# Row stores by block, an earlier load of the first token group, and a new place for row sums in a one-layer streaming encoder

## What is computed

```python
h = _rmsnorm(y, norm1_g)
fq, fk, fv, logf, gq, gk, gv, glog, gr = _project(h, w_in, ...)   # one combined projection
fox_o = _fox_prompt(fq, fk, fv, logf)        # forgetting attention, 8 heads
gla_o, S = _gla_prompt(gq, gk, gv, glog)     # gated linear attention, 4 heads
y = y + _merge(fox_o, gla_o, gr, gla_norm_g, w_out)
y = y + (silu(n @ w_gate) * (n @ w_up)) @ w_down      # n = _rmsnorm(y, norm2_g), D_FF = 2816
```

## Time and profile before

| | us |
|---|---|
| median of 3 runs | 3261.18 (3258.51 to 3264.07) |
| profiled execution, own time | 3258.25 |
| its span | 3256.5 |
| PE busy in the span | 2992.0 (92%) |
| DVE / ACT / POOL busy | 2127.7 / 1476.5 / 1332.9 |
| mean granted TensorE clock | 0.958 |

### The profile page before, as it was taken

How to read it: one execution, slowest core, us unless ns; L and a number is a source line. 1 busy time by engine, 2 the same in 40 slices (tenths; PEclk the granted TensorE clock), 3 DMA queues, 4 the chain that set the end, 5 groups by cost and what they waited for, 6 DMA issues and landing times. The chain is left out here.

```text
span 3256.5 us, 56218 instructions
## 1 busy us (share of the span) xinstructions
PE 2992.0 (92%) x21017; PEld 2761.5 (85%) x21017; DVE 2127.7 (65%) x3916; ACT 1476.5 (45%) x2998; POOL 1332.9 (41%) x1115
## 2 busy tenths in 40 slices
PE   7999998969999968599996999999999999999997
PEld 5899998957778746377775999999999999999997
DVE  6142333428999954577773777787778867787766
ACT  6253111117888842254453444444444544454443
POOL 1010033400000000322213777777778677777773
PEclk9999999989999989699997999999999999999999
DMA  5234577753332234333334655556555575556552
GB/s 127 72 126 175 192 236 247 217 123 73 75 78 59 57 88 186 108 120 120 126 111 133 186 154 148 146 150 199 146 149 150 146 209 149 146 150 183 164 148 72
DMA packets 526644, 459.52 MB, mean 141 GB/s; under 512 B 42969, under 2 KB 462102, under 8 KB 517312
## 3 DMA queue, kind: packets, MB, share of 16 engines
q1 hardware_dynamic: 510680, 402.53, 43.1%
q0 software_dynamic: 14352, 49.03, 4.6%
q10 hardware_dynamic: 1344, 4.36, 0.6%
HBM read 353.36 MB, written 102.47 MB: 140 GB/s over the span
## 5 line engine op out<-in xcount | busy, mean ns | idle before, releaser
L2605 PE MATMUL ps_ffn<-hop,wop 128*128 128x260 f32 x7392 | 985.9, 285 | 20.9 <-POOL hop L2263 17.0
L2605 PEld LDWEIGHTS ps_ffn<-hop,wop 128*128 128x128 f32 x7392 | 934.1, 191 | 22.5 <-issue 22.5
L2617 PE MATMUL ps_ffn<-aT,dsp 128*128 128x260 f32 x4224 | 599.9, 285 | 30.0 <-DVE yacc L2449 22.1
L702 PE MATMUL ps_project<-hT,wsp 128*128 128x416 f32 (+1 forms) x3000 | 603.7, 357 | 0.0
L2617 PEld LDWEIGHTS ps_ffn<-aT,dsp 128*128 128x128 f32 x4224 | 546.7, 190 | 36.8 <-issue 27.2
L702 PEld LDWEIGHTS ps_project<-hT,wsp 128*128 128x128 f32 (+1 forms) x3000 | 549.0, 186 | 24.1 <-issue 8.7
L2255 POOL TENSOR_TENSOR wop<-wsum_n,wop 128x512 fp32r<-128x512 f32 x352 | 483.0, 1372 | 134.4 <-ACT wop L2289 132.8
L2255 POOL TENSOR_TENSOR wop<-wraw_n,wop 128x512 fp32r<-128x512 f32 x264 | 362.0, 1371 | 231.3 <-ACT wop L2289 231.2
L2449 DVE TENSOR_TENSOR yacc<-ps_ffn,yacc 128x260 f32<-128x260 f32 x640 | 267.1, 422 | 142.5 <-PE ps_ffn L2617 142.0
L2289 ACT ACTIVATE wop<-wsum_n 128x512 fp32r<-128x512 f32 x352 | 222.0, 631 | 245.3 <-PE ps_ffn L2605 244.6
L2289 ACT ACTIVATE wop<-wraw_n 128x512 fp32r<-128x512 f32 x264 | 166.0, 629 | 175.5 <-PE ps_ffn L2605 165.9
(11 more groups left out here) (278 smaller groups left out, 4248.5 us busy)
## 6 DMA issues: line engine op xcount, KB each, us to landing
wsum_n<-wsum SPq DMA_DIRECT2D x352, 256.0 KB, 5.0
draw<-in_w_down_dram SPq DMA_DIRECT2D x88, 512.0 KB, 3.5
wraw_n<-in_w_gate_dram SPq DMA_DIRECT2D x132, 256.0 KB, 3.6
wraw_n<-in_w_up_dram SPq DMA_DIRECT2D x132, 256.0 KB, 3.6
zT<-zs SPq DMA_DIRECT2D x12, 1040.0 KB, 4.0
wraw<-in_w_in_dram SPq DMA_DIRECT2D x24, 512.0 KB, 5.8
hraw<-h2T SPq DMA_DIRECT2D x16, 520.0 KB, 9.0
qk_hi<-work SPq DMA_DIRECT2D x8, 1024.0 KB, 4.4
```

Source lines behind the costliest of these rows:

```text
L702: last = pe.matmul(ps[0:w, p % NB, 0:BLK], wsp[:, b, s, k, 0:w], hT[:, g * TPB:(g + 1) * TPB, v, k, :], start=k == 0 and m == 0, stop=k == ...
L2605: last = pe.matmul(product_bank(c, i), wop[:, i, w, k, :], hop[:, i, v, k, :], start=k == 0 and m == 0, stop=k == KH - 1 and m == 2)
L2617: last = pe.matmul(ps[:, 6 + n % 2, 0:FH], dsp[:, h, w, f, c * P:(c + 1) * P], aT[:, u % 2, x, f, t * FH:(t + 1) * FH], start=f == 0 and m ...
```

## The change

Three parts.

1. project: store_rows stores a tile block by block. It waits for the copy of one block, stores this block's four token tiles (three in the last block), and goes on to the next; the two tails of 72 and 32 rows follow the last block. There are five semaphores in place of one, and out_rows(n, g) waits for the store of the same block g of the tile before.
2. gla_merge and ffn: the four loads of the first group's normed rows are issued in gla_merge's loop at t = 9, behind store_h(7), and no longer at the head of ffn's queue. hraw and its semaphores live in a scope around both stages, which clears them at its end; the buffer wst shares x2's place.
3. ffn: in every up cell (s = 1) silu of J12 stands behind item 2 and not ahead of C11, and make_a of J22 behind item 4. At the three turns, sum_h of T2 stands behind item 2, low_h of T2 ahead of low_a of J11, and sum_h of T4 behind make_a of J21.

```diff
-        r_stored = sem("r_stored")
+        r_stored = [sem(f"r_stored{g}") for g in range(NB)]
...
             def store_rows(n, prompt, sample, c):
-                sp.wait_ge(rows_out, NB * (n - N_ROWS + 1))
-                full = (NT - 1) * TT
-                sp.dma_start(prompt[0:full, c:c + P].rearrange("(t p) c -> p t c", p=TT),
-                             zr[:, 0:NT - 1, :]).then_inc(r_stored, 16)
-                sp.dma_start(prompt[full:SEQ, c:c + P], zr[0:LAST_PROMPT, NT - 1, :]).then_inc(r_stored, 16)
-                sp.dma_start(sample[:, c:c + P], zr[LAST_PROMPT:TT, NT - 1, :]).then_inc(r_stored, 16)
+                for g in range(NB):
+                    sp.wait_ge(rows_out, rows_index(n, g) + 1)
+                    t0, t1 = g * TPB, min((g + 1) * TPB, NT - 1)
+                    sp.dma_start(prompt[t0 * TT:t1 * TT, c:c + P].rearrange("(t p) c -> p t c", p=TT), zr[:, t0:t1, :]).then_inc(r_stored[g], 16)
+                sp.dma_start(prompt[(NT - 1) * TT:SEQ, c:c + P], zr[0:LAST_PROMPT, NT - 1, :]).then_inc(r_stored[NB - 1], 16)
+                sp.dma_start(sample[:, c:c + P], zr[LAST_PROMPT:TT, NT - 1, :]).then_inc(r_stored[NB - 1], 16)
...
             def out_rows(n, g):
                 r = rows_index(n, g)
-                if g == 0:
-                    if n > N_ROWS:
-                        dve.wait_ge(r_stored, 48 * (n - N_ROWS))
-                    else:
-                        dve.wait_ge(p_n_stored, 48)
+                if n > N_ROWS:
+                    dve.wait_ge(r_stored[g], (48 if g == NB - 1 else 16) * (n - N_ROWS))
+                elif g == 0:
+                    dve.wait_ge(p_n_stored, 48)
...
                 if t >= 2:
                     store_h(t - 2)
+                if t == 9:
+                    sp.wait_ge(h_stored, 16 * (-(-FT // CH) + 1))
+                    for b in range(4):
+                        load_group(sp, d, 0, b)
                 if 1 <= t <= NCH:
                     store_x(t - 1)
...
             load_w(0, P1)
-            load_h(0, 0)
             load_w(0, P5)
-            load_h(0, 1)
             load_w(0, P6)
-            load_h(0, 3)
             load_w(0, P2)
-            load_h(0, 2)
...
                     if turn:
                         low_h(q, O_T1)
-                        sum_h(q, O_T2)
                     combine(c, U2)
                     combine(c, V2)
-                    silu(u, J12)
                     combine(c, C11)
                     item(c, 2)
+                    if turn:
+                        sum_h(q, O_T2)
+                    silu(u, J12)
                     item(c, 3)
                     make_a(u, J11)
                     combine(c, U3)
                     combine(c, C22)
+                    item(c, 4)
                     make_a(u, J22)
-                    item(c, 4)
-                    low_a(u, J11)
                     if turn:
                         low_h(q, O_T2)
-                        sum_h(q, O_T4)
+                    low_a(u, J11)
                     item(c, 5)
                     combine(c, C21)
                     make_a(u, J21)
+                    if turn:
+                        sum_h(q, O_T4)
                     low_a(u, J22)
```

More of the change, by code:

```diff
@@ L297, in _ @@
             sp.wait_ge(t_stored[1], 16 * 6)
-            sp.wait_ge(r_stored, 48 * NTR)
+            for g in range(NB):
+                sp.wait_ge(r_stored[g], (48 if g == NB - 1 else 16) * NTR)
             sp.wait_ge(halves_stored, 32 * 8)
@@ L1406, in gla_merge @@
         grow = sb("grow_m", [P, D])
-        wst = sb("wst", [P, 2, D])
         wsp = sb("wsp_m", [P, 2, KD, D], F32R)
@@ L1411, in gla_merge @@
         x2 = sb("x2s", [P, 2, D])
+        wst = x2
         xn = sb("xn_m", [P, D])
@@ L2063, in late_row, with load_group @@
     return items_before(NCELL) + 2 * ITEMS + (r if r >= 4 else 3 * r + 2 - ITEMS)
+def load_group(sp, d, q, b):
+    k, t = divmod(b, 2)
+    tok = q * FT + t * FH
+    sp.dma_start(d["hraw"][:, KH * k:KH * (k + 1), FH * t:FH * (t + 1)], d["h2T"][:, KH * k:KH * (k + 1), tok:tok + FH])\
+        .then_inc(d["h_come"][b], 16)
 def ffn(nc, d):
@@ L2071, in ffn @@
         grow = sb("grow_n", [TT, D])
-        hraw = sb("hraw", [P, KD, FT])
+        hraw = d["hraw"]
         hop = sb("hop", [P, NPROD, 2, KH, FH], F32R)
@@ L2094, in ffn @@
         filled, g_in = sem("filled_n"), sem("g_in_n")
-        h_come = [sem(f"h_come{b}") for b in range(4)]
+        h_come = d["h_come"]
         h_hi, h_low_v, h_low_p, h_sum = sem("h_hi_n"), sem("h_low_v"), sem("h_low_p"), sem("h_sum")
@@ L2171, in load_h @@
             def load_h(q, b):
-                k, t = divmod(b, 2)
-                if q and b == 0:
+                if b == 0:
                     sp.wait_ge(h_low_v, 3 * q)
@@ L2178, in load_h @@
                         sp.wait_ge(y_stored[r], 16 * (q - 1))
-                tok = q * FT + t * FH
-                sp.dma_start(hraw[:, KH * k:KH * (k + 1), FH * t:FH * (t + 1)], d["h2T"][:, KH * k:KH * (k + 1), tok:tok + FH])\
-                    .then_inc(h_come[b], 16)
+                load_group(sp, d, q, b)
             def load_x(q, t):
@@ L2687, in stream_step @@
     fox_sample(nc, d)
-    gla_merge(nc, d)
-    ffn(nc, d)
+    with ExitStack() as ctx:
+        sb, sem, _ = scope(nc, ctx)
+        d["hraw"] = sb("hraw", [P, KD, FT])
+        d["h_come"] = [sem(f"h_come{b}") for b in range(4)]
+        gla_merge(nc, d)
+        ffn(nc, d)
 _INS = ['x_prompt', 'x_sample', 'cache_fox_k', 'cache_fox_v', 'cache_fox_logf', 'state_gla', 'norm1_g', 'w_in', 'w_gate2',
```

## The result

The changed kernel takes 3230.23 us (median of 5 runs, 3227.11 to 3231.28) against 3261.64 us beside it: a ratio of 0.9903, 95% interval 0.9888 to 0.9917, 31.4 us less. Forecast were 3238 us, 23 less, and a range of 3225 to 3252. The sign, the range and the larger half of the working were right; the sum is short by 8 us, and one term of it was wrong in kind.

The account below looks back on a forecast made before the run. PE, busy in 92% of the span, was taken as the bound, so gains come from its idle or slow-clock time. Terms -16 - 3.5 + 0 - 4.5 + 0 + 0.7 = -23.3 us gave 3238 us at the median, range 3225 to 3252.

Parts of the forecast that it names:

- The row stores: In project, block stores remove PE's waits for row copies, then the weight-sum chain is next: -16 us (-20 to -6).
- the 20 us at stake: In project, PE's waits for row copies plus slow matmuls behind them, without the last wait at the end: 20 us.
- The lower price that the text set for the chain, 2.3 us: In project, the weight-sum chain at 10.1 us a step takes back 2.3 us; at 10.9, all 20.
- The end of project: After the last copy only the last block and tails remain to store, so the next stage starts sooner: -3.5 us.
- The head of ffn: Group 0 loaded early lets DVE's sums stand ready and shrinks POOL's 4.08 us pause: -4.5 us (-2 to -7).
- The regular cells: In ffn's regular up cells PE has no waits, DVE's work is unchanged and no add comes later: 0.
- The turns: At ffn's three turns waits move on one item; DVE's tail limits PE's win to 1.5 us each: 0 (-4.5 to +4.5).
- The added scope: Around gla_merge and ffn, clearing semaphores and meeting once more at the end costs +0.7 us (0 to 1.5).
- The sums bind: Rival, project: weight-sum step falls only from 11.2 to 10.9 us, project wins 7 us; 3247 us, chance 0.18.
- The turns pay: Rival, ffn's turns: DVE and POOL alternate better, DVE's tail shrinks, 10.5 us gained over three turns; 3227 us, chance 0.09.
- The early load does nothing: Rival, head of ffn: the weights' landing alone holds POOL and ACT, start moves by 0.5 us; 3242 us, chance 0.05.
- Slower by small pieces: Rival, project: store pieces beside every weight-sum step slow it to a mean of 12.2 us, +23 us; 3277 us, chance 0.06.

Follow-up runs that it names:

- part 1 alone: Kernel before with only the block-by-block row stores of project (all of the diff to do with r_stored): 3239.03 us, ratio 0.9915.
- part 3 alone: Kernel before with only DVE's new order in ffn, in up cells and at the three turns: 3262.44 us, ratio 0.9986.
- part 2 alone: Kernel before with only the early load of group 0's rows in gla_merge, with its scope: 3263.26 us, ratio 0.9986.
- the run with one line moved: Kernel before with only item 4's add put ahead of make_a of J22 in the up cells: 3256.80 us, ratio 0.9964.
- 52 KB: Changed kernel with each row store split into pieces of one token tile, 22 transfers per tile in place of 7: 3229.39 us, ratio 0.9883.

## Why the prediction was right, and where it was not

**The row stores.** Right in mechanism: the stalls went, the chain of weight sums was next, at the step that was forecast (10.2 us, forecast 10.1). The term was mis-sized: of the 20 us at stake 4 were given to the chain, and it took none here (project -21.7 at PE's last transpose) and 2.8 us in the execution of part 1 alone. DVE's lateness of 9 us that PE bears without a wait was in the working, but not trusted. The lower price that the text set for the chain, 2.3 us, was nearer. The stake was too small as well: it was read from one trace. In the five kept traces with one store per tile PE waits 18.4 to 22.0 us, and its last transpose in project ends at 696.95 to 702.70; the trace of before is the lowest in both. The longest waits are those of the run with part 3 alone:

```profile
PE ps_project L714 <- DVE zr L528: 22.0, 9, 7.3
```

In the nine with stores by block it ends at 674.44 to 678.09. The means are 23.5 us apart. Together with the next term that is 29 us, and part 1 alone gave 28, where 19.5 were forecast: this is more than all of the 8 us that the sum was short by.

**The end of project.** Also mis-sized, 3.5 where 5.2 were measured. By the formula of the Trainium skill ("DMA: Bandwidth & Descriptors", Anatomy of one DMA — SWDGE (gpsimd) path) the estimate was 5.7, nearer than mine; the page gives it for transfers that GpSimd issues, and these are SP's. Part of the gain, nearly 2 us, has a cause that was not in the working: the store itself became faster in pieces.

**The head of ffn.** 4.5 forecast, 3.3 in the trace of after, 4.6 (by its ratio) for part 2 alone. The bound named, POOL's pause of 4.08 us, is the place where it went.

**The regular cells.** The step that failed reads: "In regular up cells PE has no waits; DVE's work is the same, and no add comes later. 0." It asked only whether an add comes later, and not whether one comes sooner where PE waits for it. PE started item 6 late by 0.16 us and P3 by 0.07 more, in half or all of the up cells, below what the list of waits shows. In the run with one line moved make_a of J22 still takes 1.29 to 1.31 us in most regular cells, beside a POOL step that began 0.28 us earlier, and all of these cells have the short pitch: it is the add's place that counts, not make_a's length. The line gives 12 us by the ratio (7.5 to 15.7 by its interval), 4 to 8.5 by the traces; that the runs of before mostly waited in all up cells would fit both, but no trace of them is kept. In the pair of traces above the regular cells give 2.9 of the 28.5 us.

**The turns.** 0 was forecast, with the two waits moved by an item, and a tail that lets PE win at most 1.5 us. The moved wait came as forecast (3.15 us at item 5), and the tail too: DVE's adds of items 0 and 1 came no sooner. But the first turn's cost in after is the same as before to 0.4 us, and the third's 1.7 us more: +1.6 in all, within the bounds. A third wait, for low_a of J21, which ACT's rounding of T4 now holds until sum T4 is made, was not seen.

**The rest.** The added scope cannot be seen: from PE's last instruction to the end it is 15.3 to 15.8 us in the five kept traces without it and 14.8 to 15.8 in those that have it. The 2.8 us given back between project and ffn lie in the stage fox_sample, whose code is the same: 127.95 us in after, 124.36 before. They are at least in part the change's. In the nine kept traces with stores by block the DMA engines move 300 to 312 GB/s in the first 60 us of that stage, in the five with one store per tile 321 to 332, and the stage lasts 127.2 us on average against 125.3. The windows of before and of after, in the columns of the earlier trace rows:

```profile
1196.14:1256.14 60.00, 31.32 (x138) 19.86 (x139) 20.63 (x35) 10.18 (x13) 1.16 (x6) 0.72 1.01 332
...
1168.34:1228.34 60.00, 29.04 (x121) 18.10 (x122) 18.40 (x31) 7.87 (x11) 1.17 (x6) 0.68 1.00 311
```

What the row stores of an earlier stage change for these loads stays open. Other stages hide some of it: from the next stage's first load to PE's first product of ffn it is 1052.7 to 1057.7 us in the nine, 1053.2 to 1054.3 in the five.

**The rivals.** The sums bind: no; PE lost 2.8 us to them at most. The turns pay: no; they cost. The early load does nothing: no. Slower by small pieces: no, not even at 52 KB. What brought the time below the forecast was none of them, but the forecast's own first terms.

## What to carry to other kernels

A buffer that is written and read in blocks should be given back in blocks: a wait on one block of the last tile costs nothing where the wait on a whole tile stalled three engines. Where matmuls overlap, a late start leaves no wait to list; before a stage counts as free of waits, compare the pitch of like cells, where 0.25 us in every second up cell showed at once and a single moved line was worth 4 to 8.5 us by the traces and 12 by the ratio. A term that is read from one trace of before can be read too small: in other traces the same code ended its stage up to 5.8 us later. Where one engine works without a break, an order for it that shortens one wait of another engine lengthens the next; the sum of those waits did not even tell which order was faster.

## What was not expected of the hardware

The same 1.04 MB, in rows of 512 bytes, left SBUF for HBM faster in seven transfers than in three: 7.8 us against 9.65 from the last copy to the next stage's first load. And the same code of ffn has two rhythms: up cells of 15.81 and 16.06 us in turns in the trace of before, almost all of 16.05 or more in that of part 1 alone, with 4.3 us between the two in ffn (1479.6 and 1483.9). Which one a cell has goes by who is first, POOL or DVE, by some 0.02 us: a DVE step of 0.43 us takes 1.55 where POOL's step began just ahead of it.
